# Rotary stage of a two-layer encoder: the swapped sine products on VectorE, in double buffers

## What is computed

```python
def rotate(xs, ang):
    half = xs.shape[-1] // 2
    cos = jnp.cos(ang)[None, :, None, :]
    sin = jnp.sin(ang)[None, :, None, :]
    x1, x2 = xs[..., :half], xs[..., half:]
    return jnp.concatenate([x1 * cos - x2 * sin, x2 * cos + x1 * sin], axis=-1)

def apply_axial_rope(x, ang_r, ang_c):
    xf = x.astype(jnp.float32)
    out = jnp.concatenate([rotate(xf[..., :ROPE_AXIS_DIM], ang_r),
                           rotate(xf[..., ROPE_AXIS_DIM:], ang_c)], axis=-1)
    return out.astype(x.dtype)
```

## Time and profile before

| | before |
|---|---|
| median of 3 runs | 2284.45 us |
| the three runs | 2282.91, 2284.45, 2290.5 us |
| span of the profiled execution (its own time is given only by this) | 2288.4 us |
| TensorE busy | 2084.1 us, 91% |
| VectorE, ScalarE, GpSimd busy | 963.5, 884.8, 840.3 us |
| first and second rotary stage, 18 parts of VectorE | from 538 to 612 us and from 1671 to 1744 us |

### The profile page before, as it was taken

How to read it: one execution, slowest core, us unless ns; L and a number is a source line. 1 busy time by engine, 2 the same in 40 slices (tenths; PEclk the granted TensorE clock), 3 DMA queues, 4 the chain that set the end, 5 groups by cost and what they waited for, 6 DMA issues and landing times.

```text
span 2288.4 us, 39716 instructions
## 1 busy us (share of the span) xinstructions
PE 2084.1 (91%) x13792; PEld 1908.8 (83%) x13792; DVE 963.5 (42%) x1206; ACT 884.8 (39%) x1704; POOL 840.3 (37%) x769
## 2 busy tenths in 40 slices
PE   5998898889799999999979989987888999999997
PEld 5977888789799999787779778887888999988785
DVE  3105677825623332324131176677265323323222
ACT  4113434524255555422221144443333555544222
POOL 2334446436722321322222354454376212313221
PEclk8999999899999999999989999999999999999998
DMA  3211111142111111531122111111521111133312
GB/s 123 63 55 47 44 57 60 38 145 75 42 40 57 55 44 63 168 111 56 37 68 61 47 47 58 41 60 38 163 61 40 56 39 57 44 129 104 111 60 82
DMA packets 116299, 157.03 MB, mean 69 GB/s; under 512 B 12961, under 2 KB 88993, under 8 KB 116193
## 3 DMA queue, kind: packets, MB, share of 16 engines
q1 hardware_dynamic: 78480, 96.18, 14.2%
q10 hardware_dynamic: 37712, 59.52, 7.4%
HBM read 124.20 MB, written 31.46 MB: 68 GB/s over the span
## 4 chain that ended last, share of the span: by engine, by line
PE 61%; issue 16%; POOL 8%; DVE 7%; ACT 4%; POOLq 3%; DMA 1%; DVEq 0%; ACTq 0%; SPq 0%
PE ps L505 9%; PE ps L507 9%; PE ps L506 9%; PE ps L680 6%; POOL w_lo L1110 4%; PE ps L543 4%; PE ps L545 4%; PE ps L544 4%; PE ps L664 3%; PE ps L612 3%; POOL qk L1136 2%; PE ps L569 2%; PE ps L656 2%; POOLq L1163 2%; PE ps L657 2%
## 5 line engine op out<-in xcount | busy, mean ns | idle before, releaser
L1110 POOL TENSOR_TENSOR w_lo<-w_raw,w_hi 128x256 fp32r<-128x256 f32 (+2 forms) x531 | 559.1, 1057 | 1351.0 <-ACT w_hi L785 1330.2
L543 PE MATMUL ps<-w_hi,act_hi 128*128 128x256 f32 x2112 | 636.8, 302 | 48.3 <-POOL w_lo L1110 40.7
L544 PE MATMUL ps<-w_lo,act_hi 128*128 128x256 f32 x2112 | 606.8, 287 | 0.0
L545 PE MATMUL ps<-w_hi,act_lo 128*128 128x256 f32 x2112 | 606.4, 287 | 0.0
L785 ACT ACTIVATE w_hi<-w_raw 128x256 fp32r<-128x256 f32 (+2 forms) x528 | 255.0, 486 | 818.3 <-PE ps L507 366.9
L543 PEld LDWEIGHTS ps<-w_hi,act_hi 128*128 128x128 f32 x2112 | 414.6, 196 | 60.3 <-POOL w_lo L1110 35.5
L544 PEld LDWEIGHTS ps<-w_lo,act_hi 128*128 128x128 f32 x2112 | 415.0, 196 | 0.7
L545 PEld LDWEIGHTS ps<-w_hi,act_lo 128*128 128x128 f32 x2112 | 413.6, 196 | 0.0
L1438 DVE TENSOR_REDUCE st<-ps 128x1 f32<-128x512 f32 (+1 forms) x160 | 110.3, 689 | 249.3 <-PE ps L657 248.2
L901 ACT ACTIVATE pr_t<-ps 128x512 f32<-128x512 f32 x160 | 95.6, 597 | 217.5 <-PE ps L664 217.5
L1136 POOL TENSOR_TENSOR qk<-lev,qk_t 128x768 f32<-128x768 f32 (+1 forms) x72 | 148.3, 2060 | 41.4 <-ACT lev L842 41.0
(11 more groups left out here) (140 smaller groups left out, 3354.4 us busy)
## 6 DMA issues: line engine op xcount, KB each, us to landing
w_raw<-in_w_in SPq DMA_DIRECT2D x352, 128.0 KB, 2.0
proj<-stg ACTq DMA_DIRECT2D x36, 768.0 KB, 3.3
w_raw<-in_w_in SPq DMA_DIRECT2D x64, 256.0 KB, 2.6
w_raw<-in_w_branch_a SPq DMA_DIRECT2D x32, 256.0 KB, 2.5
w_raw<-in_w_branch_b SPq DMA_DIRECT2D x32, 256.0 KB, 2.5
w_raw<-in_w_out SPq DMA_DIRECT2D x32, 256.0 KB, 2.5
q<-proj ACTq DMA_DIRECT2D x8, 768.0 KB, 6.2
zb<-proj ACTq DMA_DIRECT2D x8, 768.0 KB, 7.9
```

The costliest lines, as they stand in the source:

```text
L543: mm(out, act_hi[:, k, tok], w_hi[:, k % RING, 0:BGW], start=(k == 0 and t % 2 == 0), stop=False, skip_group_check=True)
L544: mm(out, act_hi[:, k, tok], w_lo[:, k % RING, 0:BGW], start=False, stop=False, skip_group_check=True)
L545: last = mm(out, act_lo[:, k, tok], w_hi[:, k % RING, 0:BGW], start=False, stop=(k == KT - 1), skip_group_check=True)
L1110: G.tensor_tensor(w_lo[:, slot, 0:width], w_raw[:, slot, 0:width], w_hi[:, slot, 0:width].bitcast(F32), ALU.subtract).then_inc(s.w_lo_done, 1)
```

## The change

VectorE makes the swapped products itself, and GpSimd keeps only the low halves. `rot1` and `rot2` have two buffers each. The order on VectorE becomes: sum of part n, then cosine product and the two sine products of part n+1, then scaling of part n. Three semaphores, `rot_turned`, `rot_added` and `rot_free` (two ahead at the start), take the place of `rot2_ready`, `rot2_free` and of 36 waits on `dve_chain` a layer. GpSimd's waits for `tables` and `qkv_in` go. The counts per loop turn follow, `sq`, `g_qk` and `gv_row` move up by 2 x 512 elements; other lines of the diff are only wrapped differently.

```diff
-    rot1 = sb("rot1", [P, HALF], R_T + 6 * NT * DH * 4)
-    rot2 = sb("rot2", [P, HALF], R_T + 6 * NT * DH * 4 + HALF * 4)
-    sq = sb("sq", [P, 2, HALF], R_T + 6 * NT * DH * 4 + 2 * HALF * 4)
+    rot1 = sb("rot1", [P, 2, HALF], R_T + 6 * NT * DH * 4)
+    rot2 = sb("rot2", [P, 2, HALF], R_T + 6 * NT * DH * 4 + 2 * HALF * 4)
+    sq = sb("sq", [P, 2, HALF], R_T + 6 * NT * DH * 4 + 4 * HALF * 4)
...
@@ gpsimd
-            def rope_swapped(n):
-
-                t, part = n // 3, n % 3
-                heads = 8 if part < 2 else KVH
-                src, row = (q, t * D + part * HALF) if part < 2 else (kv, t * HALF)
-                pool.wait_ge(s.rot2_free, at("rot2_free"))
-                for half in range(2):
-                    G.tensor_tensor(
-                        view(rot2, half * 16, (DH, heads), (32, 2), (1, 16)),
-                        view(src, row + (1 - half) * 16, (DH, heads), (32, 2), (1, 16)),
-                        view(cs, ((part == 2) * 2 + 1) * NT * DH + t * DH + half * 16, (0, heads), (32, 2), (1, 16)),
-                        ALU.mult)
-                pool.drain().then_inc(s.rot2_ready, 1)
...
-                n = 0
                 for i in range(6 * KT):
-                    if i == ROPE_BLOCK:
-                        pool.wait_ge(s.tables, at("tables"))
-                        pool.wait_ge(s.qkv_in, at("qkv_in", 6 * 16))
-                    if (i - ROPE_BLOCK) * 3 * NT >= n * (6 * KT - ROPE_BLOCK):
-                        rope_swapped(n)
-                        n += 1
                     split(i % KT, BGW)
...
@@ vector
-            def rope(n):
+            def rope_part(n):
                 t, part = n // 3, n % 3
                 heads = 8 if part < 2 else KVH
                 src, row = (q, t * D + part * HALF) if part < 2 else (kv, t * HALF)
+                return t, part, heads, src, row
+
+            def rope_turned(n):
+
+                t, part, heads, src, row = rope_part(n)
+                buf = n % 2 * HALF
+                dve.wait_ge(s.rot_free, at("rot_free"))
+                V.tensor_tensor(view(rot1, buf, (DH, heads), (1, DH)), view(src, row, (DH, heads), (1, DH)),
+                                view(cs, (part == 2) * 2 * NT * DH + t * DH, (0, heads), (1, DH)), ALU.mult)
+                for half in range(2):
+                    last = V.tensor_tensor(
+                        view(rot2, buf + half * 16, (DH, heads), (32, 2), (1, 16)),
+                        view(src, row + (1 - half) * 16, (DH, heads), (32, 2), (1, 16)),
+                        view(cs, ((part == 2) * 2 + 1) * NT * DH + t * DH + half * 16, (0, heads), (32, 2), (1, 16)),
+                        ALU.mult)
+                last.then_inc(s.rot_turned, 1)
+
+            def rope_added(n):
+
+                heads = rope_part(n)[2]
+                turned = view(rot1, n % 2 * HALF, (DH, heads), (1, DH))
+                dve.wait_ge(s.rot_turned, at("rot_turned"))
+                V.tensor_tensor(turned, turned, view(rot2, n % 2 * HALF, (DH, heads), (1, DH)), ALU.add).then_inc(s.rot_added, 1)
+
+            def rope_scaled(n):
+
+                t, part, heads, src, row = rope_part(n)
                 stat = t * AH + part * 8 if part < 2 else NT * AH + t * KVH
...
+                dve.wait_ge(s.rot_added, at("rot_added"))
+                V.tensor_tensor(view(src, row, (DH, heads), (1, DH)), view(rot1, n % 2 * HALF, (DH, heads), (1, DH)),
+                                view(st, 4 * NSTAT + stat, (1, heads), (0, DH)), ALU.mult).then_inc(s.rot_free, 1)
...
-            dve.sem_inc(s.rot2_free, 1)
+            dve.sem_inc(s.rot_free, 2)
...
+                rope_turned(0)
                 for n in range(3 * NT):
-                    rope(n)
+                    rope_added(n)
+                    if n + 1 < 3 * NT:
+                        rope_turned(n + 1)
+                    rope_scaled(n)
                     if n in (1, 7, 13):
                         gate_columns(n // 6)
```

More of the change, by code:

```diff
@@ L140 @@
     "tensor gla head": {
-        "w_lo_done": 16, "prod_free": 10, "gla_fix": 1, "bg_free": 6, "gate_used": 1, "q_ready": 9, "k_ready":
-        9, "a_ready": 1},
+        "w_lo_done": 16, "prod_free": 10, "gla_fix": 1, "bg_free": 6, "gate_used": 1, "q_ready": 9,
+        "k_ready": 9, "a_ready": 1},
     "tensor rope background": {
@@ L145 @@
     "tensor attention group": {
-        "w_lo_done": 16, "bg_free": 6, "k_staged": 2, "q_staged": 4, "k_stack": 2, "q_stack": 8, "exp_done": 20,
-        "v_ready": 1, "pr_t_ready": 20, "o_drained": 4},
+        "w_lo_done": 16, "bg_free": 6, "k_staged": 2, "q_staged": 4, "k_stack": 2, "q_stack": 8,
+        "exp_done": 20, "v_ready": 1, "pr_t_ready": 20, "o_drained": 4},
     "tensor layer": {
         "hn_ready": 6, "turn_free": 48, "act_phase": 5, "dve_phase": 5, "pool_phase": 5, "w_lo_done": 264,
-        "drained": 66, "prod_free": 40, "gla_fix": 4, "bg_free": 66, "gate_used": 4, "q_ready": 36, "k_ready":
-        36, "a_ready": 4, "o_read": 1, "k_staged": 8, "q_staged": 16, "k_stack": 8, "q_stack": 32, "exp_done":
-        80, "v_ready": 4, "pr_t_ready": 80, "o_drained": 16, "ob_ready": 1, "merged_ready": 12},
+        "drained": 66, "prod_free": 40, "gla_fix": 4, "bg_free": 66, "gate_used": 4, "q_ready": 36,
+        "k_ready": 36, "a_ready": 4, "o_read": 1, "k_staged": 8, "q_staged": 16, "k_stack": 8, "q_stack": 32,
+        "exp_done": 80, "v_ready": 4, "pr_t_ready": 80, "o_drained": 16, "ob_ready": 1, "merged_ready": 12},
     "scalar gla projections": {
@@ L155 @@
     "scalar gla head": {
-        "w_used": 16, "w_slot0": 64, "w_slot1": 64, "w_slot2": 64, "w_slot3": 64, "gla_fix": 1, "gate_ready": 1,
-        "gate_abs": 2, "act_chain": 3, "lev_diff": 9, "stored": 32, "bg_free": 6, "gla_o": 1},
+        "w_used": 16, "w_slot0": 64, "w_slot1": 64, "w_slot2": 64, "w_slot3": 64, "gla_fix": 1,
+        "gate_ready": 1, "gate_abs": 2, "act_chain": 3, "lev_diff": 9, "stored": 32, "bg_free": 6,
+        "gla_o": 1},
     "scalar attention group": {
@@ L161 @@
     "scalar layer": {
[L162 to L166, removed]
+        "w_used": 264, "w_slot0": 1056, "w_slot1": 1056, "w_slot2": 1056, "stat_v": 3, "turned": 48,
+        "pe_phase": 5, "dve_phase": 5, "pool_phase": 5, "w_slot3": 1056, "gemm_ready": 66, "drained": 66,
+        "gla_fix": 4, "gate_ready": 4, "gate_abs": 8, "act_chain": 12, "lev_diff": 36, "stored": 288,
+        "bg_free": 66, "gla_o": 4, "qkv_in": 96, "sq_used": 18, "sil_used": 4, "neg_max": 80,
+        "pr_turned": 80, "pv_done": 80, "zb_in": 64, "m_in0": 64, "m_in1": 64},
     "gpsimd gla projections": {
@@ L175 @@
     "gpsimd layer": {
-        "w_hi_done": 264, "pe_phase": 5, "act_phase": 5, "dve_phase": 5, "param": 240, "lev_exp": 36, "prod":
-        40, "tables": 1, "qkv_in": 96, "rot2_free": 18, "group_free": 8, "pool_chain": 16, "q_turned": 32},
+        "w_hi_done": 264, "pe_phase": 5, "act_phase": 5, "dve_phase": 5, "param": 240, "lev_exp": 36,
+        "prod": 40, "group_free": 8, "pool_chain": 16, "q_turned": 32},
     "vector gla qk": {
@@ L182 @@
     "vector gla head": {
-        "dve_chain": 2, "gla_fix": 1, "gate_ready": 1, "gate_abs": 2, "gate_used": 1, "gate_log": 1, "lev_exp":
-        9, "prod": 10, "prod_free": 10, "k_ready": 9},
+        "dve_chain": 2, "gla_fix": 1, "gate_ready": 1, "gate_abs": 2, "gate_used": 1, "gate_log": 1,
+        "lev_exp": 9, "prod": 10, "prod_free": 10, "k_ready": 9},
     "vector attention group": {
@@ L189 @@
     "vector layer": {
[L190 to L194, removed]
+        "stat_sum": 1, "dve_chain": 43, "stat_root": 3, "g_in": 16, "turn_hi": 48, "pe_phase": 5,
+        "act_phase": 5, "pool_phase": 5, "gemm_ready": 66, "drained": 66, "param": 240, "gla_fix": 4,
+        "gate_ready": 4, "gate_abs": 8, "gate_used": 4, "gate_log": 4, "lev_exp": 36, "prod": 40,
+        "prod_free": 40, "k_ready": 36, "tables": 1, "sq_ready": 18, "sil_ready": 4, "k_staged": 8,
+        "k_turned": 8, "q_turned": 32, "score": 80, "pv_done": 80, "zb_ready": 4, "sig_ready": 8,
+        "rot_free": 18, "rot_turned": 18, "rot_added": 18},
 }
@@ L316, in __init__ @@
         self.tables = sem("tables")
-        self.rot2_ready = sem("rot2_ready")
-        self.rot2_free = sem("rot2_free")
+        self.rot_turned = sem("rot_turned")
+        self.rot_added = sem("rot_added")
+        self.rot_free = sem("rot_free")
         self.group_free = sem("group_free")
@@ L405, in trunk @@
     cs_raw = sb("cs_raw", [P, 2, NT, DH], R_T + 4 * NT * DH * 4)
-    rot1 = sb("rot1", [P, HALF], R_T + 6 * NT * DH * 4)
-    rot2 = sb("rot2", [P, HALF], R_T + 6 * NT * DH * 4 + HALF * 4)
-    sq = sb("sq", [P, 2, HALF], R_T + 6 * NT * DH * 4 + 2 * HALF * 4)
-    g_qk = sb("g_qk", [P, 2, DH], R_T + 6 * NT * DH * 4 + 4 * HALF * 4)
-    gv_row = sb("gv_row", [P, GV], R_T + 6 * NT * DH * 4 + 4 * HALF * 4 + 2 * DH * 4)
+    rot1 = sb("rot1", [P, 2, HALF], R_T + 6 * NT * DH * 4)
```

(9 more changed lines are left out.)

## The result

The changed kernel takes 2297.07 us, the median of four runs, against 2285.26 for the kernel before beside it: ratio 1.0048, 95% interval 1.0028 to 1.0067. It is slower, by 0.5%; 2249 was forecast.

The account below looks back on a forecast made before the run. TensorE, busy 91% of the span, was taken to lose time in the rotary stage waiting for GpSimd's splits. Saving 2 x 16.9 us plus 1.5 for the clock gave 35.3 us, hence median 2249 us, range 2242 to 2276.

Parts of the forecast that it names:

- rival 2: Rotary stage: VectorE's unbroken run shuts GpSimd out, TensorE runs dry; attention 11.5 us a layer later, 2307 us; chance 0.10.
- part 3: Rotary stage: VectorE and GpSimd block each other; each split costs VectorE 0.54 us, 25 splits 13.5 us.
- a split over 6.5 us: Sign that the forecast gain is wrong: TensorE has only three blocks, 6.5 us, in hand when a split is due.
- first lock-out: TensorE runs dry at 547.1 us until VectorE stops for block 31's copy at 558.2; 12.3 us lost.
- its third: Last lock-out worked out for the first rotary stage: TensorE dry from 604.7 to 610.4 us.
- The second: Middle lock-out worked out for the first rotary stage: TensorE dry from 576.7 to 587.4 us.
- Part 1: GpSimd keeps only 25 splits, so TensorE's own pace leaves 56.3 us from block 23 to being ready for the keys.
- Part 2: VectorE takes the 36 half-products of a layer; a query part costs 2.47 us, its own work 43.0 us.
- The tie: End of the rotary stage: VectorE has keys staged at 597.3 us, TensorE is ready at 596.9; VectorE ends it by 0.4.
- Part 4: TensorE's lowered clock after standing for the keys: without that idle time 1.5 us come back once, bounds 0 and 3.
- Rival 1: VectorE doesn't overlap its instructions in the rotary stage; 8.2 us a layer saved, 2268 us; chance 0.20.
- Rival 3: TensorE's blocks are held by something else too, weight loads or ScalarE; no change, 2284 us; chance 0.08.

Follow-up runs that it names:

- the PSUM kernel: Changed kernel, order and double buffers kept, with VectorE's sine products and their sum written to PSUM: 2256.91 us, ratio 0.9856 to the kernel before.
- the kernel with ScalarE's other order: Changed kernel, with ScalarE making the next block's high half before copying the sums out at the end of rounds 3 to 5: 2282.79 us, ratio 0.9983.
- the kernel with the old order: Changed kernel, sine products still on VectorE, but one buffer each and every part finished before the next: 2267.98 us, ratio 0.9912 to the kernel before.

## Why the prediction was wrong

The step that failed is the choice between the forecast and rival 2, in the first sentence of part 3: "The two engines block each other", one taking turns with the other. The turns were taken from the earlier trace rows, where instructions of 768 elements let GpSimd in each time. So the sum priced a split that meets VectorE at 0.54 us of VectorE's time and put TensorE's wait for it at nothing; the runs showed one request shut out for 15.4 us and another for 9.8 in each layer, and TensorE standing for 18.4 us in the first. The row that spoke for that, 8.54 us under L1509, was put aside with two arguments, and both were wrong. The first was that `rot_turned` and `rot_free` keep VectorE from being fed more than three instructions ahead. They do, and it doesn't matter: with those waits in it the run locked GpSimd out for 15.4 us. The second was that the run of L1509 had no semaphore in it. The runs here have one at most instructions. What the lock-outs had in common is that VectorE had run back to back for some 3 us or more, with no GpSimd instruction in between, when the request came (pauses of GpSimd of 3.19 us at 495.56 in the kernel before, 4.40 and 2.86 us at 544.78 and 593.64 in the changed one). In the row that let GpSimd in, it had left 1.05 us before.

The prediction had named the sign of it, "a split over 6.5 us". Rival 2 was the mechanism, with a chance of 0.10; its price was too high, 11.5 us a layer against 5.8. Its first lock-out came as worked out (12.3 us of TensorE, measured 12.6) and its third (5.7, measured 5.8). The second (10.7 us) didn't come: GpSimd's three queued splits broke VectorE's run at its start, and no pause was long enough afterwards. That alone would have left 0.8 us of the 11.5. What brings it back to 5.8 is a term that rival 2 left out, the clock: behind each of the two waits TensorE ran at 1.2 GHz, its matmuls 0.21 us apart instead of 0.12, from 560.24 to 566.52 and from 603.54 to 607.48 us. By these starts that cost 2.8 and 1.8 us, and the waits were 0.4 us longer than worked out. So TensorE's waits (18.4 us) gave back about what the move could win (17.3, from 73.5 to 56.2), and most of the loss is the clock behind them. 2 x 5.8 explains the 11.8 us between the medians.

Point by point:
- Part 1, TensorE's pace as the floor: right. Predicted 56.3 us, the kernel without rotary work and the PSUM kernel both took 56.2. This could only be seen once the lock-out was gone.
- Part 2, VectorE's own work: right. A query part was put at 2.47 us and takes 2.47 (548.74 to 551.21). Waits that are met cost nothing.
- Part 3, the price of a split that gets in: right in size. In the kernel with a gap every third part the stage was 58.1 us against 56.7. The tie wasn't one there: TensorE stood 1.8 us for the keys, so VectorE ended the stage.
- Part 4, the clock: the term exists (0.50 behind the long wait, 1.00 throughout the stage in the PSUM kernel), but it was counted only as a gain behind the wait for the keys. In the changed kernel it worked the other way, 4.6 us in the first layer.
- Rival 1, instructions that end before the next begins: fell; VectorE's starts are 0.60 us apart.
- Rival 3: fell with the kernel without rotary work.
- The forecast of 2249 was not quite reached by the two kernels with gaps in this stage alone (2260.63 and 2253.00): the sum was near under the condition that it took for granted, that a waiting split gets in at the next instruction.

What isn't settled: what exactly decides. Take the shorter of two times, GpSimd's pause and the time since VectorE's last gap, for all splits of the profiled runs that were asked for beside a run of VectorE with operands in SBUF. Up to 2.48 us every one was through within 2.9 us. From 3.06 us on every one was shut out. Between 2.6 and 3.0 us both happened, so a single threshold of time doesn't fit: 2.64 us was shut out in the kernel with ScalarE's other order, 2.65 us got in with a gap in every third part, and in the kernel with the old order this one got in beside 24 scalings of `va` in a row:

```profile
495.33 1.68 POOL L1113 TENSOR_TENSOR w_lo<-w_raw,w_hi 128x256 fp32r<-128x256 f32 x2 [2.87 <-ACT w_hi L788]
```

A number of instructions doesn't draw the line either: six or seven had begun on VectorE in the requests that got in at 2.65 and 2.87 us, and six or seven in those shut out at 2.64 and 2.86. So where in VectorE's sequence a request falls (theory B) may decide in this band; no run varied that alone. What is shown is that each long lock-out ended 0.6 us after VectorE's run did.

## What to carry to other kernels

An engine that is tuned to run without a gap can cost more than it gains when it can shut another out, as here: look for the longest single instruction of the other engine, not its mean or median, which improved here. Where the two exclude each other, plan a short gap (here one wait on the engine's own last instruction in every third rotary part, some 6.5 us apart), or put one operand into PSUM. And when a profile holds one row of the bad kind, find out what it has in common with the planned code before arguing it away.

## What was not expected of the hardware

- A request of GpSimd beside a back-to-back run of VectorE with two SBUF inputs got in soon if GpSimd had left at most 2.48 us before, and not before the end of the run, for up to 15.4 us and 31 instructions, from 3.06 us on; between 2.6 and 3.0 us either happened. In the changed kernel's rotary stage it was the same in both layers, to 0.01 us in the length of the lock-outs (15.406 and 15.412, 9.849 and 9.849).
- GpSimd's fills, which only write, ran unhindered beside the same run: 6 in 2.86 us.
- A sum and a scaling with one operand in PSUM take VectorE the same 0.68 us as in SBUF (512 elements), and a split beside them took 0.74.
- The kernel before also loses time to a lock-out of the same kind ahead of the rotary parts, under the scaling of `va`. With one gap a part, and with the old order, the request that it shuts out got in in layer 1 and was shut out for 8.1 and 8.3 us in layer 2. Six waits a layer there took back about 7 us between two kernels with operands in SBUF (2253.00 to 2246.10) and about 15 us between two with PSUM (2256.91 to 2242.17); the intervals are wide enough that the sizes may be the same.
